# Two transformer blocks on one core: SBUF buffers moved to multiples of 1024 bytes, feed-forward input chunks 272 columns apart

## The reference, cut to what matters

```
# first block
x = x + concat(norms(heads(rms_norm(x) @ w_in))) @ w_out
h = rms_norm(x);  a = gelu(h . u[e]) * gate       # e: 128 picked experts of each token
x = x + sum_e a[e] * v[e]
# second block, for each of two layers
u = rms_norm(x) * (1 + sc_a) + sh_a;  proj = u @ w_in
x = x + gt_a * ((g0 * (y_fox @ w_o_fox) + g1 * (y_mla @ w_o_mla) + g2 * (y_sb @ w_o_sb)) @ w_out)
u = rms_norm(x) * (1 + sc_f) + sh_f
x = x + gt_f * ((silu(u @ w_gate) * (u @ w_up)) @ w_down)
```

## The kernel before, in words

| buffer | start | past 1024 | past 64 |
|---|---|---|---|
| `ring`, `xT` | 1152, 25728 | 128 | 0 |
| `uT` (`u_lo` is laid over it) | 33920 | 128 | 0 |
| `cst` | 42112 | 128 | 0 |
| `sq` (`u_hi` is laid over it) | 58400 | 32 | 32 |
| `part_hi`, `part_lo` | 66592, 74784 | 32 | 32 |
| `w_hi`, `w_lo` | 82976, 85024 | 32 | 32 |
| `arena` (attention tensors, `memT`, gates) | 95520 | 288 | 32 |
| `y_hi`, `y_lo`, `m_hi`, `m_lo` (in the arena) | | 288 | 32 |
| `f_hi`, first chunk; next ones 1032 bytes apart | 177440 | 288 | 32 |
| `f_lo`, first chunk; next ones 1032 bytes apart | 185696 | 352 | 32 |

## Time and profile before

### The profile page before, as it was taken

The page is one execution under the profiler, slowest core; times in us unless marked ns, Lnnn a source line. Parts: engine busy times, 40 slices in busy tenths (PEclk is TensorE's granted clock), DMA queues, the critical chain, the costliest instruction groups (busy, mean ns, idle before and its releaser), DMA issues.

```text
span 2091.5 us, 45385 instructions
## 1 busy us (share of the span) xinstructions
PE 2025.4 (97%) x15432; PEld 1916.2 (92%) x15432; DVE 1524.3 (73%) x3577; ACT 1098.1 (53%) x2253; POOL 210.3 (10%) x218
## 2 busy tenths in 40 slices
PE   8999999879999999999999999999999999999998
PEld 7769988868999999999999889999999978899998
DVE  5766797797668888888886377876666647777666
ACT  3243655795444444444456465654445555655444
POOL 0000499681000000000000000000000000000000
PEclk9999999999999999999999999999999999999999
DMA  8345555203568777777745543445554553345553
GB/s 305 121 131 170 187 163 165 82 0 131 181 218 288 277 273 278 278 277 276 272 150 172 182 131 110 144 162 181 182 181 141 181 171 110 103 165 178 181 182 110
DMA packets 103535, 375.99 MB, mean 180 GB/s; under 512 B 11504, under 2 KB 11776, under 8 KB 103168
## 3 DMA queue, kind: packets, MB, share of 16 engines
q1 hardware_dynamic: 89280, 323.86, 46.9%
q10 hardware_dynamic: 14144, 50.72, 6.3%
HBM read 373.47 MB, written 1.05 MB: 179 GB/s over the span
## 4 chain that ended last, share of the span: by engine, by line
PE 81%; DVE 7%; issue 5%; POOL 3%; ACT 2%; DVEq 1%; DMA 0%; ACTq 0%; POOLq 0%
PE bank L767 22%; PE bank L773 21%; PE bank L770 21%; POOL part_lo L1580 3%; PE bank L569 3%; PE bank L724 1%; DVE one_hots L1872 1%; PE bank L985 1%; PE bank L941 1%; PE bank L1023 1%; PE bank L842 1%; DVE part_lo L2014 1%; PE bank L900 1%; PE bank L906 1%; PE bank L903 1%
## 5 line engine op out<-in xcount | busy, mean ns | idle before, releaser
L1214 ACT ACTIVATE part_hi<-ring 128x512 fp32r<-128x512 f32 x1108 | 681.9, 626 | 428.0 <-PE bank L770 403.3
L1707 DVE TENSOR_TENSOR part_lo<-ring,part_hi 128x512 fp32r<-128x512 f32 x712 | 473.0, 689 | 223.0 <-ACT part_hi L1214 217.4
L767 PE MATMUL bank<-u_hi,part_hi 128*128 128x256 f32 (+1 forms) x1904 | 546.8, 287 | 15.2 <-POOL part_lo L1580 10.3
L773 PE MATMUL bank<-u_hi,part_lo 128*128 128x256 f32 (+1 forms) x1904 | 534.3, 281 | 0.0
L770 PE MATMUL bank<-u_lo,part_hi 128*128 128x256 f32 (+1 forms) x1904 | 532.5, 280 | 0.0
L767 PE MATMUL bank<-w_hi,part_hi 128*128 128x256 f32 x1376 | 389.2, 283 | 3.5 <-DVE w_lo L1910 2.1
L770 PE MATMUL bank<-w_lo,part_hi 128*128 128x256 f32 x1376 | 388.6, 282 | 0.0
L773 PE MATMUL bank<-w_hi,part_lo 128*128 128x256 f32 x1376 | 388.6, 282 | 0.0
L767 PEld LDWEIGHTS bank<-u_hi,part_hi 128*128 128x128 f32 (+1 forms) x1904 | 356.4, 187 | 25.8 <-POOL part_lo L1580 12.2
L773 PEld LDWEIGHTS bank<-u_hi,part_lo 128*128 128x128 f32 (+1 forms) x1904 | 358.8, 188 | 0.5
L770 PEld LDWEIGHTS bank<-u_lo,part_hi 128*128 128x128 f32 (+1 forms) x1904 | 356.6, 187 | 1.3
(11 more groups left out here) (283 smaller groups left out, 2905.8 us busy)
## 6 DMA issues: line engine op xcount, KB each, us to landing
ring<-stream_dram SPq DMA_DIRECT2D x606, 512.0 KB, 3.4
arena<-ada_dram ACTq DMA_DIRECT2D x96, 512.0 KB, 4.6
xT<-x_dram SPq DMA_DIRECT2D x4, 256.0 KB, 6.0
arena<-mem_dram SPq DMA_DIRECT2D x1, 1024.0 KB, 9.7
arena<-keys_dram SPq DMA_DIRECT2D x1, 1024.0 KB, 6.3
out_dram<-uT SPq DMA_DIRECT2D x4, 256.0 KB, 2.5
cst<-consts_dram SPq DMA_DIRECT2D x1, 841.0 KB, 14.5
cond<-cond_dram SPq DMA_DIRECT2D x1, 512.0 KB, 15.3
```

Of the source, the lines that this page charges most:

```text
L767: m = pe.matmul(o, hi, u(cc), start=first, stop=False, **flags)
L773: m = pe.matmul(o, lo, u(cc), start=False, stop=last, **flags)
L1214: act.activation(part_hi[:, h % 4, 0:width], ring[:, n % RING, (h % 2) * width:(h % 2 + 1) * width], ACT.Copy).then_inc(hi_ready, 1)
L1707: v.tensor_tensor(part_lo[:, h % 4, :], ring[:, n % RING, (h % 2) * 512:(h % 2 + 1) * 512], part_hi[:, h % 4, :], ALU.subtract).then_inc(l ...
```

## The change

Small tensors (`cst`, `vec`, `mod`, `gmod`, `small`, `token_root`, `token_inv`, `ada_col`) are allocated first, then a filler that nothing reads or writes reaches to the next multiple of 1024 bytes. `ring`, `xT`, `uT`, `cond`, `cosT`, `sinT`, `sq`, `part_hi`, `part_lo`, `w_hi`, `w_lo`, `roots`, `act2`, `wgt2` and the arena follow; each is a multiple of 1024 bytes long. The chunks of `f_hi` and `f_lo` are 272 columns (1088 bytes, 17 x 64) apart instead of 258; the matmuls still read 258. No instruction is added or taken away.

```diff
+        cst = sb("cst", [P, C_KEEP])
+        vec = sb("vec", [P, VN])
+        mod = sb("mod", [P, NLAYER, ADA])
+        gmod = sb("gmod", [P, NLAYER, 16])
+        small = sb("small", [P, 64])
+        token_root = sb("token_root", [P, 2])
+        token_inv = sb("token_inverse", [P, 2])
+        ada_col = sb("ada_col", [P, 6])
+        sb("to_next_kilobyte", [P, (1024 - (nc.sbuf_base + 31) // 32 * 32 % 1024) // 4])
         ring = sb("ring", [P, RING, 1024])
         xT = sb("xT", [P, DC, S])
         uT_at = nc.sbuf_base
         uT = sb("uT", [P, DC, S])
-        cst = sb("cst", [P, C_KEEP])
-        vec = sb("vec", [P, VN])
-        mod = sb("mod", [P, NLAYER, ADA])
-        gmod = sb("gmod", [P, NLAYER, 16])
         cond = sb("cond", [P, D])
...
-        small = sb("small", [P, 64])
         arena_at = nc.sbuf_base
...
-        ada_col = sb("ada_col", [P, 6])
...
-        FW = S + 2
-        f_hi = nc.alloc_sbuf_tensor_at("f_hi", [P, DC, FW], F32R, offset=arena_at + 4 * gates_at)
-        f_lo = nc.alloc_sbuf_tensor_at("f_lo", [P, DC, FW], F32R, offset=arena_at + 4 * (gates_at + DC * FW))
-        assert 2 * DC * FW <= 24 * S
+        FW, FROW = S + 2, S + 16
+        f_hi = nc.alloc_sbuf_tensor_at("f_hi", [P, DC, FROW], F32R, offset=arena_at + 4 * gates_at)
+        f_lo = nc.alloc_sbuf_tensor_at("f_lo", [P, DC, FROW], F32R, offset=arena_at + 4 * (gates_at + DC * FROW))
+        assert 2 * DC * FROW <= 24 * S
...
-        token_root = sb("token_root", [P, 2])
-        token_inv = sb("token_inverse", [P, 2])
...
-                                   lambda c: f_hi[:, c, :], lambda c: f_lo[:, c, :], fresh)
+                                   lambda c: f_hi[:, c, 0:FW], lambda c: f_lo[:, c, 0:FW], fresh)
```

## The result

The changed kernel takes 2105.4 us (median of 2103.5 to 2105.7), the kernel before 2094.9 in the same comparison: ratio 1.005, interval 1.0038 to 1.0063. It is slower by 10.5 us. The forecast was 2041 us. What came is the slower rival, whose time was put at 2107; its two signs, `u_lo` at 283 ns and a `u` step of 120 ns, are both there.

What follows compares the result with a forecast made beforehand. TensorE was taken as the bound. 56.0 us for aligned streams plus 1.2 for project_tokens minus 3 for GpSimd waits gave 54 us off the 2091.5 us span, 2037.5, so 2041 for the runs; range 1975 to 2107, likeliest case 2010 to 2080.

Steps and rivals of the forecast that it cites:

- the slower rival: Passes matmuls: distance between streamed operand and weights counts, not alignment; u_lo's 1904 matmuls lose 6.3 ns each, 2107 us; chance 0.18.
- What bounds the kernel: TensorE, busy 97% of 2091.5 us; each passes matmul pays some 13 ns over its columns, about 155 us in all.
- item 1: Streamed 256-column operands become aligned: u_hi 24.0 us, w 26.0, y and m 6.0; sum 56.0 us saved.
- the reading before it: 1024 streamed bytes touch 16 pieces of 64 bytes when aligned, 17 from 32 past; an aligned operand saves 6.3 ns.
- The rival's reason: TensorE streams one operand while loading weights from the same memory; u_lo, 96 bytes off part, pays less than the others.
- The argument that put the slower rival at 0.18: Chunks of f visit many distances from part, yet its rows stay at 120 to 121 ns; some should have fallen.
- Item 2: f chunks with a stride of 272 columns: 1032 bytes touch 17 pieces either way, worth 0.
- Item 3: project_tokens streams part_hi/part_lo in 512 columns, 192 times; one piece less each, 1.2 us saved.
- Item 4: part_hi and part_lo as stationary weights become aligned: taken as 0, both ends kept for the range.
- the larger gain: Weights' alignment counts too: excess falls to 2.6 ns, steps of 109 to 110 ns, 1972 us; chance 0.17.
- Items 5 and 6: VectorE and ScalarE gain nothing from alignment; small tiles placed first, with an unused filler, change nothing.
- The 3 us given back: In 200 to 390 us, half of a 6.2 us saving turns into waits for GpSimd's low parts.

Runs made afterwards that it cites:

- run one: The changed kernel with only u_lo moved, to 96 bytes past a multiple of 1024 (32 past a multiple of 64): 2093.2 us, ratio 0.9994.
- run two: The kernel before with only u_lo moved, to 32 bytes past a multiple of 1024 like the other operands: 2104.6 us, ratio 1.0051.
- runs three: The changed kernel with gaps of 96 bytes before part and before w: 2093.0 us, ratio 0.9999.
- run eight: The changed kernel with gaps of 64 bytes before part and 96 between w_hi and w_lo: 2069.9 us, in one execution.
- Runs six: The changed kernel with all inputs 32 bytes behind part and the f chunks 512 columns apart: 2077.6 us, ratio 0.9927.
- eleven: The changed kernel with gaps of 64 bytes before part and 192 before w, f chunks 320 columns apart: 2053.7 to 2076.4 us, ratio 0.9856.
- Run twelve: The kernel before with only the f_hi and f_lo chunks set 272 columns apart: 2094.1 us, ratio 0.9995.

## Why the prediction was wrong, step by step

**What bounds the kernel** held: TensorE's matmuls made all of the difference (+13.2 us on `u` and `w`, -2.0 on `f` and `project_tokens`), the busy time of VectorE, ScalarE and GpSimd moved by less than 2 us, and no wait took its place. The excess over 106.7 ns in each matmul was rightly named as what places could change. It is 12 ns on average (155 us over 12912 matmuls); 13 is `w`'s.

**The step that failed is item 1 and the reading before it**: "a streamed operand costs one piece more when it lies across them". `u_lo` differed from the others in two ways, its place past a multiple of 64 and its place relative to `part` and `u_hi`, and I took the first for the cause. Runs one and two separate them. The size of what `u_lo` gave was right, 6.3 ns for each of its matmuls (it came as 2.1 ns on each of the three of a triple), and so was the rival's +12 us for `u`. The 56 us for `u_hi`, `w`, `y` and `m` were never there: aligned, `w` came to +1.2 us, and `u_hi` to nothing that `u_lo` didn't bring. The rival's reason was half right: a relative place it is, but runs three and eight show that it isn't `u_lo`'s distance from `part` alone, since all inputs at +96 cost as much as all at 0.

**The argument that put the slower rival at 0.18** failed too: "the chunks of `f` lie at steps of 8 bytes ... some should have fallen". Runs six and eleven show that `f` can't testify: with 258 columns even a constant distance, +32 or 192, leaves 120 ns and more. That the other operands stood at 0 and 256, which pay alike (120.0 and 119.7), was the evidence, and I had it in the prediction as the rival's "for".

**Item 2**, `f` worth 0: near (-1.0 us), but not by the pieces that I counted. Run twelve has the stride alone and the same 120.0 ns. **Item 3**, `project_tokens`: -1.0 us for 1.2, but not by alignment: run two, with all distances 0 and nothing aligned, has 227.7 ns where the aligned kernel has 227.5. With 512 columns, 0 for all is cheaper, not dearer; the agreement is luck. **Item 4**, aligned weights 0: as taken (run two, with the weights 32 past, and the changed kernel both step at 120.0); the larger gain's 109 ns didn't come, and no block in any run steps below 113.3. **Items 5 and 6**: right, as far as the busy times tell. **The 3 us given back** to GpSimd's stretch had no gain to take from.

**The pages.** No block of `passes` matmuls steps below 113.3 ns, while by the Trainium skill, "TensorE: Matmul & The Clock Gate", section "Wait — 56ns, not 53.3ns?", N/2.4 + 2.5 ns makes an estimate of 109 for 256 columns. The same page of the Trainium skill, "Step-by-step: what each phase is for", says that loading the next weights doesn't steal SBUF read bandwidth from the running matmul, since the two have ports of their own. No run here looks at a port, but for these fp32r matmuls the relative place of the two operands isn't indifferent: it moves the step from 120.0 to 113.3 ns. The 16-byte lines of the Trainium skill's "SBUF — State Buffer", section "Specifications (TRN2)", would have given a change in `f`'s odd chunks alone; the distances of all other inputs here are multiples of 16 and their prices differ.

**What stays open.** That the two streams meet at common parts of the memory which repeat every 256 bytes fits the rows with one distance, but no run looks inside; it is argued, not shown. It doesn't explain the kernel before: why 96 on the low part alone gives 117.9 and on both parts 119.6 to 120.0. Whether `u_lo`'s distance from `u_hi` does that would need kernels with the two parts apart at other distances. Open too are what starts the slower speed at 192, why `u`'s blocks alternate between the speeds in run eight, and what 258 columns do. Distances that aren't multiples of 32 weren't tried in 256 columns.

## What to carry to other kernels

Where fp32r matmuls with a weight load each run back to back, the place of the streamed operand relative to the weights was worth up to 5.6% of each here (113.3 for 120.0): measure one step from the timeline (a few dozen starts) at distances in steps of 32 bytes, in more than one block and execution, and allocate by that. Here a gap of 32 bytes before `w` with `u` behind the arena gave 2074.9 us, 0.9% under the kernel before and 1.4% under the changed one (0.9908 / 1.005), with its four executions within 4 us; a distance of 192 gave 2053 us at best and 2076 at worst. And when one operand in a trace is cheaper than its fellows, list all the ways in which it differs before choosing one: giving every buffer the same round place made `u` as dear as the dearest.

## What the hardware showed that I had not expected

- The price goes by the distance between streamed operand and weights, with 120.0 ns at 0 and 113.3 at 192, and repeats after 256 bytes in the four pairs that were seen. It doesn't go by alignment: the kernel before and run one have the same `u` step with `u_lo` at 0 and at 32 past a multiple of 64, and the changed kernel and run two have 120.0 with all at 0 and all at 32 past.
- The two parts of an input don't pay each for itself: 120.0 ns with both at 0, 120.0 with both at 96 where only `w` runs, 117.9 with one at each.
- Two speeds at one distance, 113.3 and 117.8 ns, with the change between them inside an unbroken stream of matmuls at full clock, and so executions of one kernel 20 us apart. Both speeds occur in the short executions and in the long ones; at -64 in run eight they alternate from block to block.
- Streamed in 512 columns, 0 for all operands was the best of what was seen: a step of 227.5 ns, and 232.4 with `u_lo` elsewhere.
- 258 columns instead of 256 take away the effect of a constant distance: 120.0 ns at +32, 120.8 at 192.
